# Differential attention's value product: one full fp32 matmul against three rounded ones

## The reference

```python
s = jnp.einsum('bqhmd,bkhmd->bhmqk', q.astype(f32), kd) * SCALE
...
p = jax.nn.softmax(s, axis=-1)
a = p[:, :, 0] - lam * p[:, :, 1]
return jnp.einsum('bhqk,bkhe->bqhe', a, vd)
```

## Time and profile before

| | us |
|---|---|
| median of 3 runs | 2607.64 (2605.27 to 2612.8) |
| the profiled execution | 2605.0 |
| its span, first to last instruction | 2603.2 |
| PE busy | 2478.4 (95%) |
| DVE busy | 1374.3 (53%) |
| ACT busy | 942.9 (36%) |
| POOL busy | 386.0 (15%) |

### The profile page before, as it was taken

One profiled execution on the slowest core, in us unless ns is written; L12 is line 12 of the kernel. 1 busy time (PEld: TensorE's weight loads), 2 busy tenths in 40 slices (PEclk: granted clock), 3 DMA queues, 4 the chain that ended last, 5 costly groups with the idle time before them and its releaser, 6 DMA issues.

```text
span 2603.2 us, 35097 instructions
## 1 busy us (share of the span) xinstructions
PE 2478.4 (95%) x13569; PEld 1977.2 (76%) x13569; DVE 1374.3 (53%) x2227; ACT 942.9 (36%) x1869; POOL 386.0 (15%) x398
## 2 busy tenths in 40 slices
PE   7999999999999999999988899899899989999998
PEld 5788888789999999999855565565565556888897
DVE  5311123315443333542368888788788786655553
ACT  4123331112222222111136645654664666322221
POOL 0100001121100000112352113103212242000000
PEclk9999999999999999999989999999999999999999
DMA  5688888958987666888560523235054023544432
GB/s 153 161 223 207 202 210 206 209 138 243 244 237 226 207 215 181 233 206 175 145 158 9 126 50 89 55 77 130 5 131 107 28 83 108 181 133 130 143 118 89
DMA packets 583892, 388.65 MB, mean 149 GB/s; under 512 B 318672, under 2 KB 538776, under 8 KB 577416
## 3 DMA queue, kind: packets, MB, share of 16 engines
q1 hardware_dynamic: 574592, 367.80, 53.8%
q0 software_dynamic: 9136, 18.63, 2.1%
HBM read 284.83 MB, written 134.79 MB: 161 GB/s over the span
## 4 chain that ended last, share of the span: by engine, by line
PE 75%; DVE 6%; SPq 5%; ACT 5%; issue 4%; DMA 3%; POOL 1%; DVEq 0%; ACTq 0%; POOLq 0%
PE p_acc L876 13%; PE p_acc L881 12%; PE p_acc L880 12%; PE a_op L2111 5%; PE a_sb L2086 4%; PE a_sb L2087 3%; PE a_op L2108 3%; PE a_sa L2064 2%; PE a_sa L2067 2%; PE e_U L1428 2%; PE e_U L1430 2%; PE e_U L1429 2%; ACT a_e L1924 2%; DVE a_nmax L1955 2%; PE a_sa L2065 2%
## 5 line engine op out<-in xcount | busy, mean ns | idle before, releaser
L876 PE MATMUL p_acc<-p_h_hi,p_w_hi 128*128 128x384 f32 (+1 forms) x1960 | 716.1, 365 | 11.9 <-DVE p_ev L586 5.5
L881 PE MATMUL p_acc<-p_h_hi,p_w_lo 128*128 128x384 f32 (+1 forms) x1920 | 688.0, 358 | 0.0
L880 PE MATMUL p_acc<-p_h_lo,p_w_hi 128*128 128x384 f32 (+1 forms) x1920 | 687.8, 358 | 0.0
L1955 DVE TENSOR_REDUCE a_nmax<-a_sa 128x1 f32<-128x1024 f32 (+7 forms) x384 | 347.2, 911 | 125.0 <-PE a_sa L2069 45.1
L1924 ACT ACTIVATE a_e<-a_sb 128x512 f32<-128x512 f32 (+3 forms) x640 | 310.4, 533 | 278.5 <-PE a_sb L2087 183.8
L876 PEld LDWEIGHTS p_acc<-p_h_hi,p_w_hi 128*128 128x128 f32 x1960 | 370.8, 189 | 52.7 <-issue 12.8
L881 PEld LDWEIGHTS p_acc<-p_h_hi,p_w_lo 128*128 128x128 f32 x1920 | 362.1, 189 | 30.4
L880 PEld LDWEIGHTS p_acc<-p_h_lo,p_w_hi 128*128 128x128 f32 x1920 | 362.6, 189 | 29.0
L692 DVE TENSOR_TENSOR p_w_lo<-p_raw,p_w_hi 128x1024 fp32r<-128x1024 f32 x96 | 125.6, 1308 | 368.8 <-ACT p_w_hi L619 368.7
L2086 PE MATMUL a_sb<-a_q,a_k 128*128 128x512 f32 (+2 forms) x640 | 276.5, 436 | 20.6 <-ACT a_e L1924 18.1
L2087 PE MATMUL a_sb<-a_q,a_k 68*128 68x512 f32 (+2 forms) x640 | 237.1, 374 | 0.0
(11 more groups left out here) (233 smaller groups left out, 3475.6 us busy)
## 6 DMA issues: line engine op xcount, KB each, us to landing
p_raw<-in_w_in SPq DMA_DIRECT2D x98, 512.0 KB, 5.7
s_k_raw<-scratch_kS SPq DMA_DIRECT2D x64, 512.0 KB, 6.9
scratch_kS<-in_cache_fox_k SPq DMA_DIRECT2D x32, 512.0 KB, 6.6
scratch_kS<-in_cache_diff_k SPq DMA_DIRECT2D x32, 512.0 KB, 6.4
s_v_raw<-in_cache_fox_v SPq DMA_DIRECT2D x8, 2048.0 KB, 11.0
...
```

The costliest lines, as they stand in the source:

```text
L876: nc.tensor.matmul(acc[a % 2][:, 0:n], hi, h_hi[p][:, k, at:at + n], start=(k == 0), stop=False)
L880: nc.tensor.matmul(acc[a % 2][:, 0:n], hi, h_lo[p][:, k, at:at + n], start=False, stop=False)
L881: last = nc.tensor.matmul(acc[a % 2][:, 0:n], lo, h_hi[p][:, k, at:at + n], start=False, stop=(k == DK - 1))
L1955: nc.vector.tensor_reduce(nmax[:, b % 2, c, col:col + 1], scores_of(ev[1]), axes, ALU.max, negate=True).then_inc(a_maxed, 1)
```

## The change

For differential pairs 1, 3 and 5 (`in_parts(b)`), not for 7, the weights `w` and the values `v` are each written as a rounded high part and a rounded remainder, and the product is the sum of high times high, low times high and high times low.

- Weights, per unit, event `Y(u)`, written two units after E(u): ACT casts `w` to fp32r into `w_parts[:, slot, 0]`, then POOL subtracts it from `w` into `w_parts[:, slot, 1]`. `w_parts` lies in the memory of `e`: the parts overwrite the unit's own exponentials, so an `e` slot is now free only after the product.
- Values, once per pair, event `VS(f)`, two units into the last block of the fox pair before: ACT casts the whole 128 x 2048 tile into `v_hi`, POOL writes the remainder over `v1` itself.
- Product: three fp32r matmuls; V(u-3) instead of V(u-2) in all differential pairs. The narrowest diagonal units (128 queries) are computed 256 wide, for which DVE sets 128 columns of `w` to zero (12 in all).
- Waits: `W(u)` waits for POOL's subtract of unit u-3 instead of for PE's product; E(u) waits for the product of unit u-6 instead of W(u-6). Three semaphores of the fox totals are merged into one that counts, with the same meaning.

```diff
-        e = s.sb("e", [P, E_SLOTS, MAPS, QUERIES])
+        with ExitStack() as early:
+            e = Scope(nc, early, "a_", keep).sb("e", [P, E_SLOTS, MAPS, QUERIES])
+        w_parts = s.sb("w_parts", [P, E_SLOTS, MAPS, QUERIES], F32R)
...
+    in_parts = lambda b: is_diff(b) and b // BLOCKS < FT - 1
...
             if u >= 2:
-                out.append(("R", u - 2))
+                out += [("Y", u - 2), ("R", u - 2)]
+            if b % BLOCKS == BLOCKS - 1 and u == b_first[b] + 2 and f + 1 < FT and in_parts(b + 1):
+                out.append(("VS", f + 1))
...
-            if u >= 2 and is_diff(B_UNITS[u - 2][0]):
-                multiply(u - 2)
-            elif u >= 3 and u % 2:
+            if u >= 3 and is_diff(B_UNITS[u - 3][0]):
+                multiply(u - 3)
+            if u >= 3 and u % 2 and not is_diff(B_UNITS[u - 2][0]):
                 multiply(u - 3)
                 multiply(u - 2)
...
+    def wide(u):
+        return slice(min(valid(u).start, 2 * P), QUERIES)
...
+            elif ev[0] == "VS":
+                pool.wait_ge(w_hi_made, hi_at[ev])
+                nc.gpsimd.tensor_tensor(v_lo[:], v[1][:], v_hi[:].bitcast(F32), ALU.subtract).then_inc(w_lo_made, 1)
+            elif ev[0] == "Y" and in_parts(B_UNITS[ev[1]][0]):
...
+                nc.gpsimd.tensor_tensor(w_parts[:, u % E_SLOTS, 1, cols], w[:, u % W_SLOTS, cols],
+                                        w_parts[:, u % E_SLOTS, 0, cols].bitcast(F32), ALU.subtract).then_inc(w_lo_made, 1)
...
+            elif ev[0] == "VS":
+                f = ev[1]
+                act.wait_ge(v_in[1], 16 * (f // 2 + 1))
+                nc.scalar.copy(v_hi[:], v[1][:]).then_inc(w_hi_made, 1)
+            elif ev[0] == "Y" and in_parts(B_UNITS[ev[1]][0]):
...
+                nc.scalar.copy(w_parts[:, u % E_SLOTS, 0, cols], w[:, u % W_SLOTS, cols]).then_inc(w_hi_made, 1)
...
-                dve.wait_ge(multiplied, u - W_SLOTS + 1)
+                if ("Y", u - W_SLOTS) in hi_at:
+                    dve.wait_ge(w_lo_made, hi_at["Y", u - W_SLOTS])
+                elif not in_parts(B_UNITS[u][0]):
+                    dve.wait_ge(multiplied, u - W_SLOTS + 1)
...
+            if in_parts(b):
+                cols = wide(u)
+                w_hi, w_lo = (w_parts[:, u % E_SLOTS, m, cols] for m in range(MAPS))
+                nc.tensor.matmul(op[:, cols], v_hi[:, kt, :], w_hi, start=(kt == 0), stop=False)
+                nc.tensor.matmul(op[:, cols], v_lo[:, kt, :], w_hi, start=False, stop=False)
+                last = nc.tensor.matmul(op[:, cols], v_hi[:, kt, :], w_lo, start=False, stop=final)
+            elif is_diff(b):
```

More of the change, by code:

```diff
@@ L1694, in events @@
                 out += [("MERGE", ev) for ev in link["merge"]["early"].get(u - b_first[NB - BLOCKS], [])]
-        out.append(("W", NU - 1))
-        multiply(NU - 2)
-        multiply(NU - 1)
+        out += [("W", NU - 1), ("Y", NU - 2), ("Y", NU - 1)]
+        for x in range(NU - 3, NU):
+            multiply(x)
         return head, out
@@ L1701, in prompt_attention @@
     HEAD, EVENTS = events()
+    hi_at = {}
+    for ev_ in EVENTS:
+        if ev_[0] == "VS" or ev_[0] == "Y" and in_parts(B_UNITS[ev_[1]][0]):
+            hi_at[ev_] = len(hi_at) + 1
     bank_before = {}
@@ L1917, in scalar @@
                     if m == 0 and u >= E_SLOTS:
-                        if is_diff(B_UNITS[u - E_SLOTS][0]):
+                        if is_diff(B_UNITS[u - E_SLOTS][0]) and not in_parts(B_UNITS[u - E_SLOTS][0]):
                             act.wait_ge(w_made, n_diff[u - E_SLOTS + 1])
@@ L1922, in scalar @@
                             act.wait_ge(multiplied, u - E_SLOTS + 1)
+                        if not is_diff(B_UNITS[u - E_SLOTS][0]):
                             act.wait_ge(e_added, n_added[u - E_SLOTS + (2 if B_UNITS[u - E_SLOTS][1] == 0 else 1)])
@@ L2006, in vector @@
                 dve.wait_ge(e_made, 2 * u + 2)
-                dve.wait_ge(multiplied, u - W_SLOTS + 1)
+                if ("Y", u - W_SLOTS) in hi_at:
+                    dve.wait_ge(w_lo_made, hi_at["Y", u - W_SLOTS])
+                elif not in_parts(B_UNITS[u][0]):
+                    dve.wait_ge(multiplied, u - W_SLOTS + 1)
+                if in_parts(B_UNITS[u][0]) and wide(u) != cols:
+                    nc.vector.memset(w[:, u % W_SLOTS, wide(u).start:cols.start], 0.0)
                 nc.vector.scalar_tensor_tensor(w[:, u % W_SLOTS, cols], e[:, u % E_SLOTS, 1, cols], lam[:, 5:6],
@@ L2093, in product @@
             if is_diff(b):
-                pe.wait_ge(w_made, n_diff[u + 1])
+                if in_parts(b):
+                    pe.wait_ge(w_lo_made, hi_at["Y", u])
+                else:
+                    pe.wait_ge(w_made, n_diff[u + 1])
             else:
@@ L2106, in product @@
             cols = valid(u)
-            if is_diff(b):
+            if in_parts(b):
+                cols = wide(u)
+                w_hi, w_lo = (w_parts[:, u % E_SLOTS, m, cols] for m in range(MAPS))
[3 more added lines that the diff above has]
+            elif is_diff(b):
                 last = nc.tensor.matmul(op[:, cols], v[z][:, kt, :], w[:, u % W_SLOTS, cols], start=(kt == 0), stop=final)
```

28 lines of the change are left out of this document (18 added, 10 removed).

## The result

| | before | after |
|---|---|---|
| median of the runs, us | 2606.45 (2603.14 to 2612.8, 4 runs) | 2674.70 (2671.91 to 2677.64, 4 runs) |
| ratio, 95% interval | | 1.0256 [1.0235, 1.0277] |
| span of the profiled execution, us | 2603.2 | 2675.9 |
| the four blocks of pairs 1, 3 and 5, us | 103.8, 104.3, 104.3 | 120.4, 120.6, 119.3 |
| the last fox blocks ahead of these pairs, us | 49.6, 49.6, 49.5 | 55.1, 55.1, 54.0 |

The account below looks back on a forecast made before the run. PE was taken as the main bound in blocks 1 to 3, with DVE also near its limit. 2605.0 - 16.7 + 3 + 17 + 9 = 2617.3 us, plus 2.6 for the median: 2620, range 2597 to 2646.

Parts of the forecast that it names:

- the chain sets the pace: Rival: in blocks 1 to 3 each lock wait lands on PE in full; likely +35, 2643 us; chance 0.17.
- all its terms at their upper ends: That rival's worst sum over saving, casts, lock with new chain, and values: -16.7 + 13 + 34.5 + 21 = +52 us.
- the new chain to the product: Exponentials, cast, subtract, then product: waits behind `W` at most 12 us; together with DVE's lock waits taken as 17 us.
- the DMA issues: POOL's issues of constants queue behind a subtract, up to 1.8 us late, needed some nine units later; no cost charged.
- PE's saving: Three rounded matmuls 0.235 us apart replace the fp32 product: -16.7 us if PE sets the pace everywhere.
- my prices: PE's saving per product: 0.185 us at 512 columns, 0.14 and 0.09 at 384 and 256.
- ACT's casts: 120 casts of `w`, ahead of pass A's exponential in block 1: +3 us (0 to 13).
- The lock: POOL's subtracts and DVE's two-input instructions exclude each other: 22.5 us at random meeting; with the new chain taken as 17.
- two marks: Signs of being right: POOL's 512-column subtract averages over 1.4 us, the 512-wide `W` over 0.9 instead of 0.74.
- The values: Once-per-pair split in the last fox block delays ACT's exponential and DVE's running sum: 3 us a pair (0 to 7.0), +9.
- the mark: Sign of being right: last fox blocks show a running-sum instruction over 3 us and take 2 to 5 us more.
- Pair 7: Keeps the fp32 product one unit later, which costs nothing while three slots of `w` suffice.

Follow-up runs that it names:

- e9_no_wait_for_subtract: Changed kernel, product waits only for ACT's cast; POOL's subtract still runs, its result unused (third matmul reads the high part): 2636.47 us.
- e5_shadow: Changed kernel with casts and subtracts running but unused; product is fp32 at its old place, waits for `W` alone, reads high part of values: 2633.29 us.
- e2_castfirst: Changed kernel with ACT casting unit u-2 before the exponentials of unit u instead of behind them: 2670.30 us.
- e3_values_only: Kernel before plus only the value split; the product is fp32 and reads the values' high part: 2619.28 us, 1.0039.
- e4_no_weight_split: Changed kernel without cast and subtract of weights: DVE writes `w` as fp32r, three rounded matmuls, low part left out: 2617.02 us, 1.0033.
- e6_short_subtract: Changed kernel with the weights' subtract on 128 columns instead of up to 512; third matmul reads the high part: 2640.72 us.

## Why the prediction was wrong

The direction was right, and the mechanism that decided was among the rivals ("the chain sets the pace", at 0.17); but I took it for an unlikely one, and even there 2643 was too low, as were all its terms at their upper ends (2605 + 52).

**The step that failed** is "the new chain to the product". I wrote that "the slack of the product is gone at once", and then charged only the subtract's meetings with `W`: "0.11 us a unit, 12 us over 108 units, at most". With the exponentials, cast, subtract and product closed into a loop of 4.48 us for two units, every other delay in it counts as well, and I had not listed what stands ahead of the subtract on POOL's queue. I had priced the DMA issues the wrong way round, as queued "behind a subtract"; they are queued ahead of one too, 2.02 us, and so is the fox division in block 0, for which I took 0. Measured: 23.6 us in blocks 1 to 3, all of it in blocks 2 and 3, and 12.2 in blocks 0 (after less `e9_no_wait_for_subtract`); the 7.2 us a pair that are read at full clock in both kernels would make 21.6 of the 23.6. Three groups of issues are at most 3 x 2.02 = 6.1 of the 7.9 us that blocks 1 to 3 of a pair lose; no run tried them apart, so their share is read from the chain and not shown.

**PE's saving** was right for one product and not for the pair: 0.23 us starts, as predicted, but 6.5 us over three pairs for 16.7 (8.1 if no block had lost clock). My sum took PE for the bound in all blocks. In blocks 0 and 1 it was not, and in 2 and 3 half of the price was had (22 full and six narrower products a pair at my prices are 12.8). In the kernel with everything but the chain (`e9_no_wait_for_subtract`) blocks 2 and 3 keep some of it: at full clock they take 28.8 and 36.0 us, 29.3 and 37.3 in `e5_shadow` with the heavier product. Blocks 0 and 1 lose more than that again (128.6 us for 120.8 in three pairs); in pair 3 block 1 is at granted clock 0.87 there and at 1.00 in `e5_shadow`, which may be why; it is not shown.

**ACT's casts** I took at 3 us, by pass A's exponential in block 1. `e5_shadow` has 4.8 us more in the blocks 1, with the lock in it: the place was right and the size near.

**The lock** was milder than forecast in the kernel after. I named two marks: a subtract over 1.4 us and `W` over 0.9. They came out at 1.31 and 0.86. With the casts it costs 8.3 us (`e5_shadow`), less than the 3 + 17 that I had for both and the chain. That `W` met the subtract at random was wrong as well: the order of the steps sets how they meet, as 1082 ns in `e2_castfirst` and 859 after show.

**The values** cost 5.2 us a pair by the two profiles, for the 3 that I took, within the ends 0 and 7.0. But 3.1 of the 5.5 us of a block go with the clock, which had no term, and by the medians `e3_values_only` costs 9.6 us, 3.2 a pair: this term was not what failed. The form was right: the running sum takes 4.64 us, where the mark was "over 3", and the blocks 4.5 to 5.5 us more, where it was 2 to 5. PE's idle time there did not take it up, it grew: its weight loads wait 9.1 us for pass A's exponentials in the last fox block ahead of pair 3, 6.8 before.

**The clock** had no term. Time at the lower one doubled, 61.3 to 126.0 us. It costs much where PE is the bound (7.9 against 14.1 us for one block in `e4_no_weight_split`; 49.6, 51.2 and 52.7 for the last fox block without a split, at 1.00, 0.97 and 0.94). Of the 35.8 us of the path through POOL some 21.6 are not the clock's (7.2 us a pair, read in blocks that have the full clock in both kernels). How much of the other 14.2, and of the 12.1 us that remain in the pairs, is the clock's was not tried.

**Pair 7** at V(u-3), "costs nothing": its blocks take 18.3, 24.1, 27.0 and 33.7 us for 17.5, 23.6, 26.8 and 33.1, 2.1 us more. But with the same pair 7 it takes 99.6 us in `e6_short_subtract` and 99.9 in `e9_no_wait_for_subtract`, against 101.0 before, so this is not the order's price.

The sum by what was measured: 47.9 in the pairs, of which 35.8 are the path through POOL and 12.1 what is left of casts, lock, clock and saving; 15.5 in the last fox blocks, for the values and the lower clock there; 3.5 in the first fox blocks behind the three pairs; 4.4 ahead of attention and 1.4 elsewhere, unassigned.
